# Output projection of two transformer layers as three products of split operands, in two phases over eight banks

## The chip, the cores and the metric

The kernel runs on one core of a Trainium2 chip. The metric is the device time of one execution in microseconds; three runs of the kernel before gave 2158.05, 2159.62 and 2159.68, median 2159.62. The core has five engines that run side by side and wait for each other by semaphores: TensorE (PE) for matrix products and transposes, VectorE (DVE), ScalarE (ACT), GpSimd (POOL) and SyncE (SP), which here issues most of the DMAs. Matrix products write to eight PSUM banks of 128 x 512 float32.

## The reference

A first block (mixing, attention, mixture of experts) is followed by a layer norm and two layers of a second kind, 512 rows of width 1024. The change touches these two layers alone:

```python
def hybrid_layer_2(x, p_i, positions, w_in, ..., w_o, ln1_g, ln1_b, w_gu, w_down, w_pg, w_pp, ln2_g, ln2_b):
    h = x @ w_in                                  # then split, rotated
    oa = swa_sink_attention(qa, ka, va, sinks)    # 8 windowed heads of 64
    ob = dsa_sparse_attention(qb, kb, vb, qi, ki, wi, k_top)   # 8 heads over selected keys
    mix = jnp.concatenate([oa, ob], axis=-1) @ w_o
    x = layer_norm_2(DN_ALPHA * x + mix, ln1_g, ln1_b)
    g, u = jnp.split(x @ w_gu, 2, axis=-1)
    ffn = (jax.nn.silu(g) * u) @ w_down
    ple = (p_i @ w_pp) * jax.nn.sigmoid(x @ w_pg)
    return layer_norm_2(DN_ALPHA * x + ffn + ple, ln2_g, ln2_b)
```

All is float32. A product may be done in float32 directly, or by splitting both operands into a high part (float32r, a cast) and a low part (the rest, a subtraction) and adding high x high, high x low and low x high.

## The kernel before, in words

The rows are T = 4 tiles of 128, the width C8 = 8 chunks of 128. A loop over the two layers stands in each engine's program, in the order written there; each engine works through its own list in order. `plan_layer` gives every use of a PSUM bank a place in advance: `u2.begin` makes PE wait until the bank's previous use is freed, `u2.full` tells the reader, `u2.read` waits for that, `u2.free` and `u2.evacuated` are the way back. `Sig` is a counting semaphore with its uses per layer.

Attention runs over 64 units (kind, tile, head), in the order: windowed ("a") tiles 1, 2, 3; selected ("b") tiles 1, 2, 3, 0; windowed tile 0. Units 40 to 47 are kind b, tile 3, and have 512 keys; units 48 to 63 have 128. For each pair of units PE makes the scores (L2285, mask products L2292 or L2296). DVE takes each unit's row maximum (L1829) and after the second the negated pair (L1834 or L1837). ACT makes the exponential (L1263) once the pair's negation is there. PE transposes the probabilities three units later (L2304), ACT copies them (`take_pt`, L1252), and PE multiplies them by the values one unit after (L2315). In ACT's list, unit n is: `take_pt(n - 3)`, then the exponential of n. After a group of eight, DVE divides and evacuates the output (`take_o`, L1849 and L1851). DVE also picks the largest index scores in this loop (`pick`, L1807, L1808), up to unit 37.

Then PE transposes the heads' outputs (`oT`, 8 chunks, L2216), ACT copies them to `HT` (L1180), and once all are there PE makes the output projection `mix` in float32 (L2343): for each tile and half width 8 products of 128 x 128 by 128 x 512. For each tile DVE adds the residual (L1897), takes the statistics (L1694, L1696), POOL the reciprocal root (L974, L975), and DVE normalises (L1700, L1702). PE transposes the tile (`x1T`), ACT casts the high part (`split_x1`, L1193) and DVE subtracts the low part (L1873). `w_pg` is loaded by SP after `p` and `w_pp` (L860 to L862), once oT 0 is full; ACT casts its 8 chunks (L1281) after tile 0's split and DVE subtracts them (L1907) after tile 2's normalisation. PE ends the stage with two transposes of p (`plT`), 16 products of p with `w_pp` in 8 banks (`pp`, L2357), tile 3's transposes, and the gate product (`pg`), already done as three products by `split_product` (L244 to L246). After it comes the feed-forward part, also split.

Of the kernel before, what the change touches and what calls it, by code (L numbers as in the profile page):

```python
# [6 lines left out]
P = 128  # L7
F32, F32R, BF16, I32 = mybir.dt.float32, mybir.dt.float32r, mybir.dt.bfloat16, mybir.dt.int32
ALU = mybir.AluOpType
# [29 lines left out]
IN2 = 1704  # L39
# [30 lines left out]
HEAD_TAPS = 87  # L70
FILLERS = 2
PICKS_A, PICKS_B, PICKS_C = 18, 29, 29
PICK_AT = [3, *range(7, 34, 2), 34, 35, 36, 37]
# [104 lines left out]
def plan_layer(before):  # L178
# [36 lines left out]
    b.next = 0  # L215
    for j in range(C8):
        b.take(("oT", j))
    for t in range(T):
        for half in range(2):
            b.take(("mix", t, half))  # L220
        if t:
            for half in range(2):
                b.take(("x1T", t - 1, half))
    for c in range(2):
        b.take(("plT", c))
    for t in range(T):
        for half in range(2):
            b.take(("pp", t, half))
    for half in range(2):
        b.take(("x1T", T - 1, half))  # L230
    for t in range(T):
# [17 lines left out]
def build(nc, i, out, stop=None):  # L249
    ctx = ExitStack()  # L250
    with ctx:
# [248 lines left out]
        PT2 = at(o + 4 * S, 3, S)  # L500
        assert o + 7 * S <= offB + C8 * sum(b - a for a, b in IN_CUTS[1:4])

        pg_hi = part("w_pg_hi", offB, C8, D)
# [9 lines left out]
        o = offB + C8 * IN2  # L513
        w_o2 = at(o, C8, D)
        gu_hi = [part(f"gate_up_hi{n}", o + 4 * D + n * 2 * D, 2, C8, P) for n in range(2)]
# [184 lines left out]
        y_xhi = Sig("x1_high_parts", 2 * T)  # L700
        y_ghi = Sig("w_pg_high_parts", C8)
        y_glo = Sig("w_pg_low_parts", C8)
        y_dhi = Sig("down_high_parts", FC)
# [48 lines left out]
        def _(sp):  # L752
# [79 lines left out]
            with sp.Fori(0, LAYERS) as l:  # L832
# [24 lines left out]
                sp.dma_start(lnB, of("ln1_b_2").rearrange("a n -> (a n)").partition_broadcast(P)).then_inc(d_ln1, 16)  # L857
                u2.read(sp, ("oT", 0), l)
                apart(sp)
                sp.dma_start(p_in, of("p_2").rearrange("l b (t p) n -> (l b p) t n", p=P)).then_inc(d_pp, 16)  # L860
                sp.dma_start(w_pp, of("w_pp_2").rearrange("a (c p) n -> (a p) c n", p=P)).then_inc(d_pp, 16)
                sp.dma_start(w_pg, of("w_pg_2").rearrange("a (p c) n -> (a p) c n", c=C8)).then_inc(d_pg, 16)  # L862
                u2.read(sp, ("mix", T - 1, 1), l)
# [127 lines left out]
        def _(act):  # L991
# [179 lines left out]
            with act.Fori(0, LAYERS) as l:  # L1171
# [74 lines left out]
                def take_pt(n):  # L1246
# [5 lines left out]
                    u2.free(act.copy(PT2[:, n % 3, 0:w], ps[:, 0:w]), ("pT", kind, t, h))  # L1252

                for n, (kind, t, h) in enumerate(UNITS):
                    w = width(n)
                    kk = 0 if kind == "a" else 1
                    if n >= 3:
                        take_pt(n - 3)
                    y_neg.wait(act, l, n // 2 + 1)
                    if n >= 4:  # L1260
                        u2.evacuated(act, ("pT",) + UNITS[n - 4], l)
                    ps = u2.read(act, ("s", kind, t, h), l)
                    u2.free(act.activation(Pr2[:, n % 4, 0:w], ps[:, 0:w], ACT.Exp, bias=nmx2[:, kk, t, h:h + 1],  # L1263
                                           scale=HD ** -0.5, accum_out=ls2[:, kk, t, h:h + 1]), ("s", kind, t, h))
                    if n < T - 2:
                        take_in(n + 2, 4)
                    if n in TURN_AT:
                        key = TURNED[TURN_AT[n]]
                        take_turned(key, turned[key])
                    if kind == "a" and h == 7:  # L1270
                        y_sinkd.wait(act, l, WINDOWED.index(t) + 1)
                        y_sinke.inc(act.activation(es2[:, t], es2[:, t], ACT.Exp))
                for n in range(len(UNITS) - 3, len(UNITS)):
                    take_pt(n)
                for j in range(C8):
                    take_turned(("oT", j), HT[:, j])
                split_x1(0)
                act.wait_ge(d_pg, 16 * (l + 1))
                apart(act)
                for c in range(C8):  # L1280
                    y_ghi.inc(act.copy(pg_hi[:, c], w_pg[:, c]))  # L1281
                for t in range(1, T - 1):
                    split_x1(t)
                for c in range(2):
                    take_turned(("plT", c), pT[:, c])
                for t in range(T):
                    for half in range(2):
                        take_turned(("pp", t, half), PLB[:, t, 512 * half:512 * half + 512])
                split_x1(T - 1)
                gate_up_high(0, 0)  # L1290
# [25 lines left out]
        def _(dve):  # L1316
# [402 lines left out]
            with dve.Fori(0, LAYERS) as l:  # L1719
# [123 lines left out]
                def take_o(kind, t):  # L1843
                    kk = 0 if kind == "a" else 1
                    u2.evacuated(dve, ("s", kind, t, 7), l)
                    if kind == "a":
# [5 lines left out]
                                              rl2[:, kk, t].unsqueeze(2).broadcast_to([P, 8, HD]), ALU.mult), ("o", kind, t))  # L1852

                for n in range(len(UNITS) + 3):
                    if n < len(UNITS):
                        row_max(n)
                    if n == 4:
                        u2.all_evacuated(dve, [("in", t, 4) for t in range(T)], l)
                        y_rot.wait(dve, l, 5)
                        rotate(heads_of(KB, 1, HD), [KBD[:, :, n:n + 1] for n in range(2)], c32, s32, 1, 32, copies=2)  # L1860
                    if n in PICK_AT:
                        pick(PICKS_C + PICK_AT.index(n))
                    if n >= 4 and (n - 3) % 8 == 0:
                        take_o(*UNITS[n - 4][:2])
                take_o(*UNITS[-1][:2])

                def split_x1(t):
# [24 lines left out]
                for t in range(T):  # L1892
# [9 lines left out]
                    if t:  # L1902
                        split_x1(t - 1)
                    if t == T - 2:
                        for c in range(C8):
                            y_ghi.wait(dve, l, c + 1)
                            y_glo.inc(dve.tensor_tensor(pg_lo[:, c], w_pg[:, c], pg_hi[:, c].bitcast(F32), ALU.subtract))  # L1907
                split_x1(T - 1)
# [40 lines left out]
        def _(pe):  # L1949
# [262 lines left out]
            with pe.Fori(0, LAYERS) as l:  # L2212
# [108 lines left out]
                for n in range(len(UNITS) + 4):  # L2321
# [8 lines left out]
                    if n in TURN_AT:  # L2330
                        turn_heads([TURNED[TURN_AT[n]]])
                for j in range(C8):
                    if j % 4 == 0:
                        u2.all_evacuated(pe, [("o", "ab"[j // 4], t) for t in range(T)], l)
                    turn2(("oT", j), [O2[:, j // 4, t, (j % 4) * P:(j % 4 + 1) * P] for t in range(T)])
                for j in range(C8):
                    u2.evacuated(pe, ("oT", j), l)
                pe.wait_ge(d_o2, 16 * (l + 1))
                for t in range(T):
                    for half in range(2):  # L2340
                        ps = u2.begin(pe, ("mix", t, half), l)
                        for m in range(C8):
                            ins = pe.matmul(ps[:], HT[:, m, t * P:(t + 1) * P], w_o2[:, m, 512 * half:512 * half + 512], start=m == 0, stop=m == C8 - 1)  # L2343
                        u2.full(ins, ("mix", t, half))
                    if t:
                        y_x1.wait(pe, l, t)
                        tile("x1T", t - 1)

# [4 lines left out]
                for t in range(T):  # L2353
                    for half in range(2):
# [3 lines left out]
                        u2.full(ins, ("pp", t, half))  # L2358
                y_x1.wait(pe, l, T)
                tile("x1T", T - 1)  # L2360
                y_glo.wait(pe, l, C8)
                u2.all_evacuated(pe, [("x1T", t, half) for t in range(T) for half in range(2)], l)
# [60 lines left out]
```

## Time and profile before

| | us |
|---|---|
| median of three runs | 2159.62 |
| profiled execution | 2162.41 |
| its span | 2160.3 |
| PE busy | 1968.9 (91%) |
| DVE busy | 1124.6 (52%) |
| ACT busy | 725.5 (34%) |
| POOL busy | 149.1 (7%) |

Times of the trace count from the start of the span. A busy time is the union of the records of an engine; matmul records overlap, so the duration of one is longer than its step in a row of them. A float32 matmul is recorded as two instructions. An idle time in brackets stands before the instruction, with the line that released it. The clock in the table of stretches is the one granted to PE, as a share of 2.4 GHz.

### The profile page before, as it was taken

The page shows a single profiled execution, that of the slowest core. Times are in us where ns is not written, and L with a number is a line of the kernel's source. Part 1 is how long each engine was busy: PE and PEld are TensorE (multiplying, and loading weights), DVE is VectorE, ACT ScalarE, POOL GpSimd, SP SyncE. Part 2 cuts the span into 40 slices and gives each one's busy share as a digit, 9 for nine tenths or more (in the row PEclk, how much of TensorE's full clock was granted, in tenths as well). Part 3 has the DMA queues.
Part 4 walks back from the last instruction along what each step waited for, and adds up shares of the span by engine and source line. Part 5 has one row for each costly group of instructions (what it writes and reads, how often), then busy time and mean ns, then how long its engine had stood idle before and what let it go on. Part 6 is the DMA issues. An engine that isn't in the chain of part 4 may idle for free.

```text
span 2160.3 us, 25297 instructions
## 1 busy us (share of the span) xinstructions
PE 1968.9 (91%) x8610; PEld 1397.3 (65%) x8614; DVE 1124.6 (52%) x1828; ACT 725.5 (34%) x1222; POOL 149.1 (7%) x157
## 2 busy tenths in 40 slices
PE   4997994799998698999999999999889999999995
PEld 2445644666665455655788887865566478888784
DVE  2787625688886788635222222367872522222235
ACT  2034421455554234533233332213353313333221
POOL 1000001133332100000000000010000000000001
PEclk9999996899999799999999999999999999999998
DMA  9162104699995700022033342250002103334220
GB/s 378 55 230 81 68 10 147 220 366 357 353 358 187 297 3 1 21 108 59 20 97 97 97 136 86 94 178 9 1 21 108 39 20 98 97 97 155 68 88 39
DMA packets 148060, 267.17 MB, mean 124 GB/s; under 512 B 11456, under 2 KB 108736, under 8 KB 134784
## 3 DMA queue, kind: packets, MB, share of 16 engines
q1 hardware_dynamic: 141776, 256.29, 33.6%
q0 software_dynamic: 6192, 9.70, 1.4%
q8 instruction: 51, 0.84, 0.2%
q14 instruction: 41, 0.34, 0.1%
HBM read 257.57 MB, written 20.97 MB: 129 GB/s over the span
## 4 chain that ended last, share of the span: by engine, by line
PE 78%; DVE 13%; issue 3%; ACT 2%; DMA 2%; POOL 1%; SPq 0%; DVEq 0%; ACTq 0%; POOLq 0%
PE bank L244 15%; PE bank L245 15%; PE bank L246 15%; PE bank L2343 5%; PE bank L2184 5%; PE bank L2228 5%; PE bank L2000 3%; DVE arena L1808 3%; PE bank L2089 2%; DVE arena L1807 2%; PE bank L1976 1%; PE bank L2315 1%; PE bank L2357 1%; DVE arena L1829 1%; DMA arena<-w_ada 1%
## 5 line engine op out<-in xcount | busy, mean ns | idle before, releaser
L244 PE MATMUL bank<-ht_hi,gate_up_hi 128*128 128x512 f32 x704 | 274.1, 389 | 2.8 <-ACT arena L1297 2.8
L245 PE MATMUL bank<-ht_lo,gate_up_hi 128*128 128x512 f32 x704 | 273.9, 389 | 0.0
L246 PE MATMUL bank<-ht_hi,gate_up_lo 128*128 128x512 f32 x704 | 273.9, 389 | 0.0
L2228 PE MATMUL bank<-arena 128*128 128x512 f32 (+3 forms) x640 | 194.9, 464 | 11.5 <-ACT arena L1186 6.4
L1623 DVE TENSOR_TENSOR expert_gate_up_lo<-expert_gate_up,expert_gate_up_hi 128x2048 fp32r<-128x2048 f32 x64 | 146.6, 2292 | 57.8 <-ACT expert_gate_up_hi L1113 55.2
L1884 DVE TENSOR_TENSOR arena<-arena,bank 128x512 f32 (+1 forms) x44 | 30.2, 687 | 272.0 <-ACT arena L1205 272.0
L2228 PEld LDWEIGHTS bank<-arena 128*128 128x128 f32 x640 | 114.7, 196 | 85.9 <-issue 64.3
L244 PEld LDWEIGHTS bank<-ht_hi,gate_up_hi 128*128 128x128 f32 x704 | 132.2, 188 | 31.2 <-issue 3.7
L246 PEld LDWEIGHTS bank<-ht_hi,gate_up_lo 128*128 128x128 f32 x704 | 132.2, 188 | 27.5
L245 PEld LDWEIGHTS bank<-ht_lo,gate_up_hi 128*128 128x128 f32 x704 | 132.2, 188 | 27.1
L1113 ACT CAST expert_gate_up_hi<-expert_gate_up 128x2048 fp32r<-128x2048 f32 x64 | 121.6, 1902 | 71.7 <-PE bank L246 71.6
L244 PE MATMUL bank<-down_hi,product_hi 128*128 128x512 f32 x352 | 138.2, 393 | 3.5 <-DVE arena L1884 3.5
L246 PE MATMUL bank<-down_hi,product_lo 128*128 128x512 f32 x352 | 138.1, 392 | 0.0
L245 PE MATMUL bank<-down_lo,product_hi 128*128 128x512 f32 x352 | 138.0, 392 | 0.0
L1878 DVE TENSOR_TENSOR gate_up_lo<-gate_up_whole,gate_up_hi 128x2048 fp32r<-128x2048 f32 x44 | 100.9, 2292 | 67.4 <-ACT gate_up_hi L1199 66.8
L1888 DVE TENSOR_TENSOR down_lo<-down_whole,down_hi 128x1024 fp32r<-128x1024 f32 x44 | 53.9, 1224 | 157.7 <-ACT product_hi L1213 157.7
L974 POOL TENSOR_SCALAR arena<-arena 128x1 f32<-128x1 f32 x20 | 23.1, 1157 | 1388.7 <-DVE arena L1696 1388.7
L2184 PE MATMUL bank<-arena 128*128 128x512 f32 x256 | 115.1, 592 | 0.7 <-ACT arena L1135 0.7
L2343 PE MATMUL bank<-arena 128*128 128x512 f32 x256 | 111.1, 593 | 1.7 <-ACT arena L1180 1.7
L244 PE MATMUL bank<-expert_gate_up_hi,window_hi 128*128 128x512 f32 x256 | 103.8, 405 | 2.8 <-DVE window_lo L1646 2.8
L1211 ACT CAST down_hi<-down_whole 128x1024 fp32r<-128x1024 f32 x44 | 46.1, 1048 | 164.1 <-PE bank L246 164.1
L245 PE MATMUL bank<-expert_gate_up_lo,window_hi 128*128 128x512 f32 x256 | 101.1, 395 | 0.0
(334 smaller groups left out, 3383.6 us busy)
## 6 DMA issues: line engine op xcount, KB each, us to landing
gate_up_whole<-w_gu SPq DMA_DIRECT2D x88, 512.0 KB, 5.1
expert_gate_up<-w_gate_e SPq DMA_DIRECT2D x32, 1024.0 KB, 6.9
expert_gate_up<-w_up_e SPq DMA_DIRECT2D x32, 1024.0 KB, 9.5
arena<-w_down_e SPq DMA_DIRECT2D x32, 1024.0 KB
down_whole<-w_down SPq DMA_DIRECT2D x44, 512.0 KB, 3.5
arena<-w_ada SPq DMA_DIRECT2D x5, 4096.0 KB, 20.6
arena<-w_in SPq DMA_DIRECT2D x4, 2048.0 KB, 16.0
arena<-w_o SPq DMA_DIRECT2D x2, 4096.0 KB, 13.0
```

The lines of the kernel that those rows point to most:

```text
L244: pe.matmul(ps, xh, wh, start=start, stop=False)
L245: pe.matmul(ps, xh, wl, start=False, stop=False)
L246: return pe.matmul(ps, xl, wh, start=False, stop=stop)
L1113: act.copy(ring_hi[half], ring[s][:, :, 4 * half:4 * half + 4]).then_inc(m_whi, 1)
L1623: dve.tensor_tensor(ring_lo[s][:, :, c4], ring[s][:, :, c4], ring_hi[half].bitcast(F32), ALU.subtract).then_inc(m_wlo, 1)
L1808: own.link(dve.match_replace(sc, top8, sc, TAKEN))
L1878: dve.tensor_tensor(gu_lo[s], gu[s], gu_hi[s].bitcast(F32), ALU.subtract).then_inc(f_lo, 1)
L1888: dve.tensor_tensor(dn_lo[f % 2], w_dn[:, f % DN_SLOTS], dn_hi[f % 2].bitcast(F32), ALU.subtract)
L2000: ins = pe.matmul(ps[:], w_in[:, c, c0 + m * P:c0 + (m + 1) * P], HT[:, c], start=c == 0, stop=c == C8 - 1)
L2184: ins = pe.matmul(bank[4 + 2 * (s % 2) + half][:], AT[:, s % 2, c], ring_d[s % 2][:, c, 512 * half:512 * half + 512], start=c == 0, stop=c ...
L2228: ins = pe.matmul(ps[:, 0:b - a], HT[:, c, t * P:(t + 1) * P], w_in2[j][:, c], start=c == 0, stop=c == C8 - 1)
L2343: ins = pe.matmul(ps[:], HT[:, m, t * P:(t + 1) * P], w_o2[:, m, 512 * half:512 * half + 512], start=m == 0, stop=m == C8 - 1)
```

## The change

The output projection becomes three products of split operands, as the gate product is. `w_o` is loaded as before. Its chunks 4 to 7 (`OUT_FIRST`, the selected heads) are split inside attention: at units 41, 43, 45 and 47 ACT casts one (`out_high`, after that unit's exponential) and DVE subtracts (`out_low`, after that unit's row maximum). Chunks 0 to 3 (`OUT_LAST`) are split after the heads. The low part is written in place of the loaded weight; the high parts lie in room that is free by then. The heads are transposed in the order 4 to 7, 0 to 3; ACT casts each to `HT_hi`, DVE subtracts to `HT_lo`, from the same bank.

The projection runs in two phases: for all eight (tile, half) banks the chunks 4 to 7, then for all eight the chunks 0 to 3. The x1 transposes of tile t come after tile t + 2 of the second phase, for tiles 2 and 3 inside the small products of p. On SP, `w_pg` is issued right behind `p` once the first transposed head is full, and `w_pp` waits until the first tile of the projection is full. ACT's casts of `w_pg` come ahead of all x1 splits, and DVE's subtractions of it ahead of the first evacuation of the projection.

```diff
+OUT_FIRST, OUT_LAST = range(4, 8), range(4)
+OUT_SPLIT_AT = {41 + 2 * k: m for k, m in enumerate(OUT_FIRST)}
...
-    for j in range(C8):
+    for j in [*OUT_FIRST, *OUT_LAST]:
         b.take(("oT", j))
     for t in range(T):
         for half in range(2):
             b.take(("mix", t, half))
-        if t:
-            for half in range(2):
-                b.take(("x1T", t - 1, half))
+    for t in range(T - 2):
+        for half in range(2):
+            b.take(("x1T", t, half))
     for c in range(2):
         b.take(("plT", c))
     for t in range(T):
         for half in range(2):
             b.take(("pp", t, half))
-    for half in range(2):
-        b.take(("x1T", T - 1, half))
+        if t % 2:
+            for half in range(2):
+                b.take(("x1T", T - 2 + t // 2, half))
...
-                u2.read(sp, ("oT", 0), l)
+                u2.read(sp, ("oT", OUT_FIRST[0]), l)
                 apart(sp)
                 sp.dma_start(p_in, of("p_2").rearrange("l b (t p) n -> (l b p) t n", p=P)).then_inc(d_pp, 16)
+                sp.dma_start(w_pg, of("w_pg_2").rearrange("a (p c) n -> (a p) c n", c=C8)).then_inc(d_pg, 16)
+                u2.read(sp, ("mix", 0, 0), l)
+                apart(sp)
                 sp.dma_start(w_pp, of("w_pp_2").rearrange("a (c p) n -> (a p) c n", p=P)).then_inc(d_pp, 16)
-                sp.dma_start(w_pg, of("w_pg_2").rearrange("a (p c) n -> (a p) c n", c=C8)).then_inc(d_pg, 16)
...
+                def out_high(m):
+                    act.wait_ge(d_o2, 16 * (l + 1))
+                    y_ghi.inc(act.copy(w_o2_hi[m], w_o2[:, m]))
...
+                    if n in OUT_SPLIT_AT:
+                        out_high(OUT_SPLIT_AT[n])
...
-                for j in range(C8):
-                    take_turned(("oT", j), HT[:, j])
-                split_x1(0)
+                for j in [*OUT_FIRST, *OUT_LAST]:
+                    ps = u2.read(act, ("oT", j), l)
+                    y_ghi.inc(act.copy(HT_hi[:, j], ps[:]))
+                for m in OUT_LAST:
+                    out_high(m)
...
+                def out_low(m):
+                    y_ghi.wait(dve, l, (OUT_FIRST.index(m) if m in OUT_FIRST else OUT_LAST_HI + OUT_LAST.index(m)) + 1)
+                    y_glo.inc(dve.tensor_tensor(w_o2_lo[:, m], w_o2[:, m], w_o2_hi[m].bitcast(F32), ALU.subtract))
...
+                    if n in OUT_SPLIT_AT:
+                        out_low(OUT_SPLIT_AT[n])
...
+                for k, j in enumerate([*OUT_FIRST, *OUT_LAST]):
+                    ps = u2.read(dve, ("oT", j), l)
+                    y_ghi.wait(dve, l, HEADS_HI + k + 1)
+                    ins = dve.tensor_tensor(HT_lo[:, j], ps[:], HT_hi[:, j].bitcast(F32), ALU.subtract)
+                    u2.free(ins, ("oT", j))
+                for m in OUT_LAST:
+                    out_low(m)
+                for c in range(C8):
+                    y_ghi.wait(dve, l, PG_HI + c + 1)
+                    y_glo.inc(dve.tensor_tensor(pg_lo[:, c], w_pg[:, c], pg_hi[:, c].bitcast(F32), ALU.subtract))
...
+                def mix(t, half, ms):
+                    key = ("mix", t, half)
+                    ps = u2.begin(pe, key, l) if ms is OUT_FIRST else bank[b2.where[key][0]]
+                    ts, cs = slice(t * P, (t + 1) * P), slice(512 * half, 512 * half + 512)
+                    for m in ms:
+                        ins = split_product(pe, ps[:], (HT_hi[:, m, ts], HT_lo[:, m, ts]), (w_o2_hi[m][:, cs], w_o2_lo[:, m, cs]),
+                                            m == OUT_FIRST[0], m == OUT_LAST[-1])
+                    if ms is OUT_LAST:
+                        u2.full(ins, key)
+
+                for ms in (OUT_FIRST, OUT_LAST):
+                    y_glo.wait(pe, l, 4 if ms is OUT_FIRST else C8)
+                    for j in ms:
+                        u2.evacuated(pe, ("oT", j), l)
+                    for t in range(T):
+                        for half in range(2):
+                            mix(t, half, ms)
+                        if ms is OUT_LAST and t > 1:
+                            y_x1.wait(pe, l, t - 1)
+                            tile("x1T", t - 2)
```

## Rows read from the trace of the kernel before

**Rows 1.** The page's part 4: shares of the chain that ended last.
```profile
PE 78%; DVE 13%; issue 3%; ACT 2%; DMA 2%; POOL 1%; SPq 0%; DVEq 0%; ACTq 0%; POOLq 0%
```
**Rows 2.** Grouped by form, PE: line, shapes, count | busy us, mean ns | idle.
```profile
L2343 PE MATMUL bank<-arena 128*128 128x512 f32 x128 | 55.5, 593 | 0.8 <-ACT arena L1180 0.8
...
L244 PE MATMUL bank<-w_pg_hi,ht_hi 128*128 128x512 f32 x64 | 25.3, 395 | 2.0 <-DVE ht_lo L1873 2.0
```
**Rows 3.** Timeline of PE, heads' transposes to gate product: start us, us, what.
```profile
934.46 5.80 PE L2216 MATMUL bank<-arena 128*128 128x128 f32 x32 [0.79 <-DVE arena L1851]
941.10 27.73 PE L2343 MATMUL bank<-arena 128*128 128x512 f32 x64 [0.83 <-ACT arena L1180]
...
1000.73 14.00 PE L2357 MATMUL bank<-arena 128*128 128x512 f32 x32 [0.90 <-ACT arena L1180]
1014.56 1.04 PE L2216 MATMUL bank<-arena 128*128 128x128 f32 x8
1017.55 0.49 PE L244 MATMUL bank<-w_pg_hi,ht_hi 128*128 128x512 f32 x1 [1.95 <-DVE ht_lo L1873]
...
1651.15 27.73 PE L2343 MATMUL bank<-arena 128*128 128x512 f32 x64 [0.83 <-ACT arena L1180]
```
**Rows 4.** Timeline of DVE, same stretch: one tile's steps and the gate split.
```profile
968.87 0.69 DVE L1897 SCALAR_TENSOR_TENSOR arena<-arena,bank 128x512 f32<-128x512 f32 x1 [6.18 <-PE bank L2343]
...
974.56 1.28 DVE L1873 TENSOR_TENSOR ht_lo<-bank,ht_hi 128x512 fp32r<-128x512 f32 x2
...
990.38 9.16 DVE L1907 TENSOR_TENSOR w_pg_lo<-w_pg_whole,w_pg_hi 128x1024 fp32r<-128x1024 f32 x8
```
**Rows 5.** Timeline of ACT, same stretch: the casts of the gate weight.
```profile
970.27 7.67 ACT L1281 CAST w_pg_hi<-w_pg_whole 128x1024 fp32r<-128x1024 f32 x8
```
**Rows 6.** Timeline of PE at the 512-key units: two pairs' scores, unit 45's values.
```profile
906.59 1.13 PE L2285 MATMUL bank<-arena 64*128 64x512 f32 x4
...
910.75 1.13 PE L2285 MATMUL bank<-arena 64*128 64x512 f32 x4
...
917.18 1.00 PE L2315 MATMUL bank<-arena 128*128 128x64 f32 x8
```
**Rows 7.** Timeline of DVE there: negation, output group, next two row maxima, negation.
```profile
905.80 0.17 DVE L1837 TENSOR_SCALAR arena<-arena 128x2 f32<-128x2 f32 x1
905.88 0.20 DVE L1849 RECIPROCAL arena<-arena 128x8 f32<-128x8 f32 x1
906.70 0.69 DVE L1851 TENSOR_TENSOR arena<-bank,arena 128x512 f32<-128x512 f32 x1 [0.62 <-PE bank L2315]
908.08 1.29 DVE L1829 TENSOR_REDUCE arena<-bank 128x1 f32<-128x512 f32 x2 [0.69 <-PE bank L2292]
909.40 0.17 DVE L1837 TENSOR_SCALAR arena<-arena 128x2 f32<-128x2 f32 x1
```
**Rows 8.** Timeline of ACT there: copy, exponential, copy, exponential.
```profile
905.08 0.48 ACT L1252 COPY arena<-bank 128x384 f32<-128x384 f32 x1 [1.07 <-PE bank L2304]
906.08 0.69 ACT L1263 ACTIVATE arena<-bank,arena 128x512 f32<-128x512 f32 x1 [0.53 <-DVE arena L1837]
...
906.76 0.58 ACT L1252 COPY arena<-bank 128x512 f32<-128x512 f32 x1
907.23 0.70 ACT L1263 ACTIVATE arena<-bank,arena 128x512 f32<-128x512 f32 x1
```
**Rows 9.** Stretches: length, busy PE, PEld, DVE, ACT, POOL, granted clock, DMA share, GB/s.
```profile
902.00:920.00 18.00, 17.95 (x143) 14.57 (x144) 6.64 (x19) 11.89 (x32) 0.00 (x0) 1.00 0.01 2
...
932.00:940.00 8.00, 7.12 (x39) 6.75 (x38) 0.72 (x2) 3.65 (x9) 0.00 (x0) 0.58 0.27 96
...
1017.00:1063.00 46.00, 44.63 (x192) 35.97 (x192) 7.51 (x10) 7.18 (x10) 0.00 (x0) 1.00 0.08 23
```
**Rows 10.** SP's timeline, then DMA issues by line: KB each, us to landing.
```profile
937.24 0.42 SPq L862 DMA_DIRECT2D w_pg_whole<-w_pg  x1
...
w_pg_whole<-w_pg SPq DMA_DIRECT2D x1, 4096.0 KB, 15.2
```

More of the change, by code:

```diff
@@ L501, in build @@
         assert o + 7 * S <= offB + C8 * sum(b - a for a, b in IN_CUTS[1:4])
+        o_turned = o - offB
         pg_hi = part("w_pg_hi", offB, C8, D)
@@ L513, in build @@
         o = offB + C8 * IN2
-        w_o2 = at(o, C8, D)
+        w_o2 = part("w_o_whole", o, C8, D, dt=F32)
+        w_o2_lo = part("w_o_lo", o, C8, D)
+        w_o2_hi = {**{m: part(f"w_o_hi{m}", offB + 9 * D + (m - 4) * D, D) for m in OUT_FIRST},
+                   **{m: part(f"w_o_hi{m}", H0 + m * D, D) for m in OUT_LAST}}
+        assert 9 * D >= o_turned + 7 * S and 13 * D <= C8 * IN2
         gu_hi = [part(f"gate_up_hi{n}", o + 4 * D + n * 2 * D, 2, C8, P) for n in range(2)]
@@ L700, in build @@
         y_xhi = Sig("x1_high_parts", 2 * T)
-        y_ghi = Sig("w_pg_high_parts", C8)
-        y_glo = Sig("w_pg_low_parts", C8)
+        y_ghi = Sig("w_o_heads_w_pg_high_parts", 3 * C8)
+        y_glo = Sig("w_o_w_pg_low_parts", 2 * C8)
+        HEADS_HI, OUT_LAST_HI, PG_HI, PG_LO = 4, 4 + C8, 2 * C8, C8
         y_dhi = Sig("down_high_parts", FC)
@@ L1281, in _ @@
                     y_ghi.inc(act.copy(pg_hi[:, c], w_pg[:, c]))
-                for t in range(1, T - 1):
+                for t in range(T - 2):
                     split_x1(t)
@@ L1288, in _ @@
                         take_turned(("pp", t, half), PLB[:, t, 512 * half:512 * half + 512])
-                split_x1(T - 1)
+                    if t % 2:
+                        split_x1(T - 2 + t // 2)
                 gate_up_high(0, 0)
@@ L1903, in _ @@
                         split_x1(t - 1)
[L1904 to L1907, printed above, removed]
                 split_x1(T - 1)
@@ L2331, in _ @@
                         turn_heads([TURNED[TURN_AT[n]]])
-                for j in range(C8):
+                for j in [*OUT_FIRST, *OUT_LAST]:
                     if j % 4 == 0:
@@ L2335, in _ @@
                     turn2(("oT", j), [O2[:, j // 4, t, (j % 4) * P:(j % 4 + 1) * P] for t in range(T)])
[L2336 to L2347, printed above, removed]
+                def mix(t, half, ms):
[17 more added lines that the diff above has]
+                            tile("x1T", t - 2)
                 pe.wait_ge(d_pp, 32 * (l + 1))
@@ L2358, in _ @@
                         u2.full(ins, ("pp", t, half))
-                y_x1.wait(pe, l, T)
-                tile("x1T", T - 1)
-                y_glo.wait(pe, l, C8)
+                    if t % 2:
+                        y_x1.wait(pe, l, T - 1 + t // 2)
+                        tile("x1T", T - 2 + t // 2)
+                y_glo.wait(pe, l, PG_LO + C8)
                 u2.all_evacuated(pe, [("x1T", t, half) for t in range(T) for half in range(2)], l)
```

## The prediction

> **What bounds the kernel now.** I read the chain of work that ended last first: TensorE (PE) carries most of it [rows 1], so a cut in PE work can pay only where PE is the last to be ready, and added work on ScalarE (ACT) or VectorE (DVE) costs only where PE then waits. The grouped instructions of two stretches give the price of the two product forms [rows 2]. The timeline of PE from the end of attention to the gate product shows a nearly unbroken PE [rows 3]: transposes of the heads, the output projection (64 float32 products, each recorded as two instructions), the x1 transposes, the small projection of p, and the gate product. The timelines of DVE and ACT over the same time show what follows each tile [rows 4, 5]. Then I read the three engines where the change puts new work into attention, at the widest units [rows 6 to 8]: PE is busy 17.95 of 18.00 us there, ACT 11.89 and DVE 6.64 [rows 9]. The second layer repeats the first 710.05 us later [rows 3], so a layer's sum counts twice.
>
> **Price of the products.** Before: 55.5 us for the 128 recorded instructions, 0.867 us a float32 product [rows 2]. After: 64 x 3 = 192 products of the gate product's shape and type. That stage has 64 of each of the three kinds; a record lasts 395 ns with its overlap [rows 2], so I take the stretch: 192 of them in 44.63 us of PE [rows 9], thus 0.2325 us each and 44.6 us in all. PE work falls by 10.9 us a layer. The row is the same operation on the same shapes, so I give this term no more than 0.5 us either way.
>
> By the Trainium skill ("FP8 and Floating Point Precision", section "TensorE Precision Notes") true FP32 takes four passes through the array. Three passes in place of four would save 55.5 / 4 = 13.9 us; this case's ratio, 0.867 to 0.2325, is 3.73 passes, so the trace agrees only roughly. With the page's figure the final estimate would be 6.0 us lower, 2145.8.
>
> **From the heads' transposes to the gate product, layer 0.** The transposes start at 934.46, 0.79 after a wait for the last windowed output [rows 3]. The selected heads now go first and need none of it: start 933.7, the 32 transposes at their 5.80 us, end 939.5. Their high part on ACT takes the place of a copy of equal size; the low part on DVE is one 128x512 subtraction, 0.65 us as in the x1 split (1.28 us for two [rows 4]). DVE has the last head of the first four split about 1.5 us after its transposes, some 938.2, so the first phase starts at 939.5 rather than 941.10. It takes 96 x 0.2325 = 22.3 us: 961.8.
> In the shadow of this phase, ACT does the last two heads, 4 weight casts (7.67 us for 8, so 0.96 each [rows 5]) to about 944, DVE 4 weight subtractions (9.16 us for 8, 1.145 each [rows 4]) to about 946. w_pg was issued at 937.24 and landed 15.2 us later [rows 10]. Its issue moves about 1.5 us ahead, and w_pp (1 MB of the 5.5 MB in that burst) is no longer in front: 948 to 951. ACT's 8 casts end at 956 to 959, DVE's 8 subtractions about a microsecond later. The first tile of the second phase is full at 961.8 + 12 x 0.2325 = 964.6. So the gate split, which before stood 9.16 us in DVE between tiles [rows 4], costs nothing; if the load came more than 3 us late, DVE would evacuate late by the excess. SP now waits for that tile before it issues w_pp, which PE wants only at about 987; no transfer behind it comes late.
> Second phase: 5.58 us a tile. Tiles end at 967.4, 973.0, 978.5; the x1 transposes (1.04 us as recorded, with the overlap at their end [rows 3]; I take 0.9) end at 979.4; the last tile 985.0, x1 transposes 985.9, p's two transposes 986.8. DVE is now what is late: from the evacuation of a tile's second half to its normalised rows it takes 974.56 - 968.87 = 5.69 us, the first half adds 0.65, the x1 split 1.3 [rows 4]. That is 7.6 us a tile against 5.58 (6.5 with x1's transposes) on PE. Tile 0 done 973.1; tile 1 979.5; split to 980.8; tile 2 987.1; split to 988.4; first half of tile 3 evacuated 989.1; tile 3 done 994.7. The first small product needs that bank (the plan gives it bank 6): it starts at 989.1, a new wait of 2.3 us. Then 14.0 us of small products [rows 3], 0.9 for tile 2's transposes: tile 3's transposes start at 1004.0. In the trace they start at 1014.56 and the gate product 2.99 us later at 1017.55 [rows 3]; kept so, the gate product starts at 1007.0. **Gain: 10.5 us a layer**, with bounds 9 (the DVE chain 1.5 worse) and 12.5 (the 2.3 us wait absent).
>
> **What attention pays.** At units 41, 43, 45, 47 ACT gets a 1024-column cast (0.96 us pitch, about 1.05 until a waiter sees it) and DVE the subtraction of it (1.15). The trace of before has no such pair here. The lower bound is nothing, if both lie in idle time; this counts as a loss or zero, since nothing is removed from this stretch. The idle shares invite that reading. But both engines work in order: the subtraction stands before the next two row maxima, and waits for the cast, which stands behind the exponential of the pair before. That closes a loop: row maxima, negation, exponential, cast, subtraction, next row maxima. One turn from negation end to negation end, by the rows: 0.11 to the exponential (905.97 to 906.08), 0.68 to the copy (906.76), 0.47 to the second exponential (907.23), 0.68 for it, cast 1.05, hand-over 0.1, subtraction 1.15, two row maxima 1.32 (908.08 to 909.40), negation 0.17 [rows 7, 8]. Sum 5.73 us, against PE's pair of 4.16 (906.59 to 910.75 [rows 6]).
> Followed through: the first cast fits the idle 1.07 us ahead of 905.08 [rows 8], its subtraction ends at 906.2 instead of leaving DVE free from 904.5, so the negation at 905.80 ends 1.7 late. At unit 43 the evacuation of a finished output group (reciprocal and multiply, 0.20 and 0.69, with the link between them 0.9 [rows 7]) stands behind the second subtraction too. The negation of 44/45 ends at 907.7 + 5.7 + 0.9 = 914.3 (before 909.57), that of 46/47 at 920.1, with the last cast from 922.0 to 923.0. PE's values of unit 45, in the trace at 917.18 [rows 6], need a probability copy behind this cast: 923.65. PE has used up its lead and is **6.5 us late**; one more copy on ACT makes 6.9. From there the narrow units run at their old pace and give nothing back. I take 6.7, with 3 (half of the loop hidden by lead that I count too small) and 9 (the loop plus slower handovers) as bounds.
>
> **Sum.** -10.5 + 6.7 = -3.8 us a layer, -7.6 for two. The profiled execution took 2162.4 us (span 2160.3), 2.8 above the median of the runs, 2159.6; its own sum gives 2154.8, and the same difference on the median gives **2152.0 us**.
>
> **Rivals.** (1) *The casts and subtractions are covered.* If the order on ACT leaves PE fed, attention pays at most 3 us a layer and the kernel gains 15 to 21 us: 2138.5 to 2144.6. For it: the idle shares [rows 9] and the first cast's 1.07 us hole. Against: DVE's wait sits ahead of row maxima that PE and ACT need next. Chance 0.20.
> (2) *TensorE falls to half clock in attention: slower.* In 932 to 940 the granted clock is 0.58 on average, that is partly 1.2 GHz, after PE's work had thinned; before, with 17.95 of 18.00 us busy, it is 1.00 [rows 9]. The loop thins PE to 4.16 of 5.73 us. If the clock falls there, each microsecond of full-clock PE work that is on the path costs one more. The gain of 3.8 us a layer is gone after 3.8 us of such work. Most of the 21 us of PE work from 912 to 934 would cost 6 to 12 more a layer: 2164 to 2176. Against it: while the loop is last, slower PE work partly fits its waits, and once it is saturated the clock comes back, as at 940. Chance 0.10.
> The Trainium skill ("TensorE: Matmul & The Clock Gate", section "A second HAM failure mode: psum-queue depth-cycling") tells of a kernel whose short idles between groups of matmuls made the gate oscillate. Followed here it would be rival 2; the rows show one such fall at the end of attention and do not show it in the wide units.
> (3) *Both prices land at their bad ends* (gain 9, loss 8 to 9, or one short fall of the clock): within 0.2%, 2156 to 2163. Chance 0.14.
> That the change does not do what it says I count within these: the operand layouts are those of the gate product.
>
> **Chances.** The forecast, 2147 to 2156, has 0.56, nearly all of it faster by over 0.2% (below 2155.3); 0.04 of it lies within 0.2%, about what a measurement of this kernel can tell from no change. Faster 0.52 + 0.20 = 0.72; same 0.04 + 0.14 = 0.18; slower 0.10. The range leaves out the lower end of rival 1 and all of rival 2: 2140 to 2162.
>
> **What would show it.** Right: 192 output products at 0.2325; the gate split finished before the first evacuation; a 2 us wait of the first small product on DVE; the stretch from the heads' transposes to the gate product near 73 us (83.1 before); PE idle 1 to 2 us at several points between units 43 and 49, released by ACT's copies, and DVE row maxima 5.7 us apart by pair. Wrong: an attention stretch as long as before, row maxima 4.2 us apart (rival 1), or a granted clock near one half between units 41 and 63 (rival 2). A w_pg load that lands after 954, or a phase that waits for a bank, would make the first term wrong.

## The result, and the profile after

The changed kernel takes 2169.64 us (median of 6 runs, 2167.97 to 2175.43), the kernel before 2159.65 beside it: ratio 1.0047, 95% interval 1.0035 to 1.0060, slower by 10 us. Forecast were 2152.0, with 2140 to 2162 as the range. The profiled execution took 2169.38 us, its span is 2167.6, so 7.3 more than the span before, and its mean granted clock 0.949 (0.962 before).

The projection itself went as the sum said. Grouped by form, its products in layer 0 (the counterparts of [rows 2]):

```profile
L247 PE MATMUL bank<-w_o_hi,ht_hi 128*128 128x512 f32 x64 | 25.1, 392 | 0.0
L249 PE MATMUL bank<-w_o_hi,ht_lo 128*128 128x512 f32 x64 | 24.9, 390 | 0.0
L248 PE MATMUL bank<-w_o_lo,ht_hi 128*128 128x512 f32 x64 | 24.9, 389 | 0.0
```

PE's timeline, in parts, from the heads' transposes to the gate product (against [rows 3]):

```profile
946.34 5.75 PE L2248 MATMUL bank<-arena 128*128 128x128 f32 x32
951.85 0.47 PE L247 MATMUL bank<-w_o_hi,ht_hi 128*128 128x512 f32 x1
...
1000.74 8.83 PE L2398 MATMUL bank<-arena 128*128 128x512 f32 x16 [2.40 <-DVE arena L1933]
1009.41 1.05 PE L2248 MATMUL bank<-arena 128*128 128x128 f32 x8
1010.29 7.03 PE L2398 MATMUL bank<-arena 128*128 128x512 f32 x16
1017.16 1.04 PE L2248 MATMUL bank<-arena 128*128 128x128 f32 x8
1020.00 0.47 PE L247 MATMUL bank<-w_pg_hi,ht_hi 128*128 128x512 f32 x1 [1.79 <-DVE ht_lo L1909]
```

From transposes to gate product it is 1020.00 - 946.34 = 73.66 us, where 83.09 stood before. The new wait of p's first product for DVE's evacuation is there, 2.40 us.

The loss lies in front of it. The same timeline at the wide units and after them (against [rows 6]):

```profile
905.00 1.13 PE L2317 MATMUL bank<-arena 64*128 64x512 f32 x4
...
907.73 1.10 PE L2347 MATMUL bank<-arena 128*128 128x64 f32 x8 [0.63 <-ACT arena L1263]
...
910.79 1.13 PE L2317 MATMUL bank<-arena 64*128 64x512 f32 x4
...
914.23 1.10 PE L2347 MATMUL bank<-arena 128*128 128x64 f32 x8 [1.33 <-ACT arena L1263]
...
916.33 1.85 PE L2347 MATMUL bank<-arena 128*128 128x64 f32 x8 [0.55 <-ACT arena L1263]
918.11 0.80 PE L2317 MATMUL bank<-arena 64*128 64x128 f32 x4
```

A pair of wide units takes 910.79 - 905.00 = 5.79 us (4.16 before), with short waits for ACT's probability copies. Then, from about 917, each group of eight value products takes 1.85 us where it took 1.1. The clock says why. Busy times and granted clock by stretch, columns as in [rows 9]:

```profile
904.00:916.00 12.00, 9.34 (x63) 6.35 (x60) 5.78 (x11) 6.44 (x14) 0.00 (x0) 1.00 0.00 0
916.00:920.00 4.00, 3.67 (x19) 3.16 (x19) 2.41 (x4) 1.71 (x5) 0.00 (x0) 0.56 0.00 0
920.00:948.00 28.00, 28.00 (x139) 24.22 (x139) 9.19 (x33) 13.64 (x56) 0.00 (x0) 0.50 0.01 2
948.00:952.00 4.00, 4.00 (x27) 4.00 (x26) 3.26 (x5) 2.97 (x7) 0.00 (x0) 0.67 0.72 264
952.00:976.00 24.00, 24.00 (x107) 19.83 (x107) 15.71 (x16) 12.35 (x14) 0.00 (x0) 1.00 0.36 154
```

PE is busy 9.34 of 12.00 us, then falls to 1.2 GHz (0.50) and stays there for 28 us, up to and into the heads' transposes, although it shows no idle time in them. It rises during these transposes (0.67 on average in 948 to 952; the projection begins at 951.85) and is at 2.4 GHz in the projection. Layer 1 has the same fall, 0.50 from 1640 to 1664, again ended inside the transposes, which start at 1661.85. In the kernel before, the clock fell only at the end of this part of attention ([rows 9], 0.58 in 932 to 940).

The balance, in us; a layer's stretches are cut at PE's scores of units 42/43, at the heads' transposes and at the gate product:

| | before, layer 0 / 1 | after, layer 0 / 1 |
|---|---|---|
| scores 42/43 to transposes | 31.47 / 31.55 | 44.94 / 44.14 |
| transposes to gate product | 83.09 / 83.00 | 73.66 / 72.67 |
| both | 114.56 / 114.55 | 118.60 / 116.81 |

This is +4.0 and +2.3 us. The span's other 1.0 us is the balance of stretches that the change does not touch: 1.6 less ahead of unit 42 of layer 0, 2.2 more between the first gate product and layer 1's unit 42, 0.4 more at the end. The spread of the same kernel from run to run is larger than that (2157.10 to 2161.97 in six runs of the kernel before).

### The profile page after: what moved, and what is told of

Read it like the earlier page. It is cut to its first block, busy times and chain, and to the rows that moved or that the text cites. A ratio compares the mean times of both kernels' runs of the same rounds, so it can differ in the third digit from the quotient of the medians.

```text
span 2167.6 us, 25637 instructions
## 1 busy us (share of the span) xinstructions
PE 1974.7 (91%) x8742; PEld 1443.0 (67%) x8742; DVE 1153.9 (53%) x1860; ACT 740.1 (34%) x1238; POOL 149.2 (7%) x157
## 4 chain that ended last, share of the span: by engine, by line
PE 76%; DVE 13%; issue 3%; DMA 3%; ACT 2%; POOL 1%; SPq 0%; DVEq 0%; ACTq 0%; POOLq 0%
PE bank L247 16%; PE bank L248 16%; PE bank L249 16%; PE bank L2216 5%; PE bank L2260 4%; PE bank L2032 3%; DVE arena L1828 2%; PE bank L2121 2%; DVE arena L1827 2%; DMA arena<-w_in 2%; PE bank L2347 2%; DVE arena L1849 1%; PE bank L2398 1%; PE bank L2008 1%; PE bank L2317 1%
## 5 line engine op out<-in xcount | busy, mean ns | idle before, releaser
L2260 PEld LDWEIGHTS bank<-arena 128*128 128x128 f32 x640 | 115.4, 198 | 85.3 <-issue 62.9
L2216 PE MATMUL bank<-arena 128*128 128x512 f32 x256 | 115.1, 592 | 0.7 <-ACT arena L1146 0.7
L2347 PE MATMUL bank<-arena 128*128 128x64 f32 x544 | 97.6, 313 | 19.4 <-ACT arena L1263 19.3
L2347 PEld LDWEIGHTS bank<-arena 128*128 128x128 f32 x544 | 86.2, 227 | 31.4 <-ACT arena L1263 22.8
```

The source lines that it names most:

```text
L2216: ins = pe.matmul(bank[4 + 2 * (s % 2) + half][:], AT[:, s % 2, c], ring_d[s % 2][:, c, 512 * half:512 * half + 512], start=c == 0, stop=c ...
L2260: ins = pe.matmul(ps[:, 0:b - a], HT[:, c, t * P:(t + 1) * P], w_in2[j][:, c], start=c == 0, stop=c == C8 - 1)
L2347: ins = pe.matmul(ps[:, h * HD:(h + 1) * HD], PT2[:, n % 3, k * P:(k + 1) * P], v, start=k == 0, stop=k == nk - 1)
```

## Experiments

In what follows, "attention's stretch" runs from the scores of units 42/43 to the heads' transposes, and "the stage" from these transposes to the gate product; two numbers are layer 0 and layer 1. Every ratio is to the kernel before, measured beside the run.

Theory: all of the loss is in attention; half of it is the closed loop of waits (cast, subtraction, row maxima) and half the clock that falls after the loop has thinned PE's work. Rivals: the load of casts and subtractions costs in any order; the projection stage's new order costs; the clock fell for another reason.

**Splits taken out of attention (e1).** In both loops over the units the call is removed, and all eight chunks stand behind the heads:

```diff
-                    if n in OUT_SPLIT_AT:
-                        out_high(OUT_SPLIT_AT[n])
...
-                for m in OUT_LAST:
+                for m in [*OUT_FIRST, *OUT_LAST]:
                     out_high(m)
```

> The change, with the casts and subtractions of chunks 4 to 7 of w_o taken out of attention and put behind the heads' splits. Theory A (what made the change slower sits in attention alone: the closed loop of cast, subtraction and row maxima, and the half clock that follows it): the 512-key units return to 4.2 us a pair, the stretch from the scores of units 42/43 to the heads' transposes to 31.5 us (44.9 in the changed kernel), at full clock; the first phase starts about 5 us later after the transposes than in the changed kernel, since 4 casts and 4 subtractions stand in front of it. About 2149 to 2154, faster than before. Rival B (the projection stage's new order costs the time: gate split first, DVE late, new waits): the time stays near 2170 or rises by the 10 us that the later start costs.

Measured: 2156.09 us, ratio to the kernel before 0.9983 (0.9966 to 0.9999). Attention's stretch is 30.61 and 30.03 us, 0.9 and 1.5 less than in the kernel before. The stage is 82.0 and 81.4: the first phase waits for DVE.

```profile
941.84 0.77 PE L247 MATMUL bank<-w_o_hi,ht_hi 128*128 128x512 f32 x1 [6.75 <-DVE w_o_lo L1874]
...
943.25 0.63 PE L247 MATMUL bank<-w_o_hi,ht_hi 128*128 128x512 f32 x1
```

That is 8.3 and 8.8 us more than in the changed kernel, not 5, and the time is 2 us above the range expected: the wait is 6.75 us (7.51 in layer 1) and the first products behind it are at half clock (records of the first kind, every third product, stand 1.28 us apart, 0.68 once the clock is full). The loss is in attention; but moving the work behind it gives back most of what the projection gains.

**Subtraction one pair later (e2).** Casts stay at units 41, 43, 45, 47; DVE's subtractions go to 43, 45, 47, 49, one pair of units behind their casts:

```diff
+OUT_LOW_AT = {43 + 2 * k: m for k, m in enumerate(OUT_FIRST)}
...
-                    if n in OUT_SPLIT_AT:
-                        out_low(OUT_SPLIT_AT[n])
+                    if n in OUT_LOW_AT:
+                        out_low(OUT_LOW_AT[n])
```

> The change, with each subtraction in attention one pair of units later (43, 45, 47, 49) and the casts left at 41, 43, 45, 47: the same work, but DVE never waits for a cast. Theory A1 (the loop of waits, not the load, is what attention pays): row maxima 4.2 us apart, PE fed, clock full, stretch from scores 42/43 to the transposes 31.5 to 33 us, time 2136 to 2142. Rival A2 (the load on ACT and DVE delays PE in any order): the stretch stays above 38 us, time 2155 or more.

Measured: 2136.63 us, ratio 0.9891 (0.9854 to 0.9928). Same work, other order, 33 us less than the changed kernel. The timeline of DVE shows the first three subtractions right behind a negation, without a wait; the fourth waits 0.46 us for its cast. PE in the same 12 us is busy all the time and at full clock:

```profile
904.03 0.17 DVE L1858 TENSOR_SCALAR arena<-arena 128x2 f32<-128x2 f32 x1
904.11 1.22 DVE L1877 TENSOR_TENSOR w_o_lo<-w_o_whole,w_o_hi 128x1024 fp32r<-128x1024 f32 x1
905.25 0.20 DVE L1870 RECIPROCAL arena<-arena 128x8 f32<-128x8 f32 x1
905.57 0.69 DVE L1872 TENSOR_TENSOR arena<-bank,arena 128x512 f32<-128x512 f32 x1
906.31 1.29 DVE L1850 TENSOR_REDUCE arena<-bank 128x1 f32<-128x512 f32 x2
907.64 0.17 DVE L1858 TENSOR_SCALAR arena<-arena 128x2 f32<-128x2 f32 x1
907.71 1.22 DVE L1877 TENSOR_TENSOR w_o_lo<-w_o_whole,w_o_hi 128x1024 fp32r<-128x1024 f32 x1
910.47 1.29 DVE L1850 TENSOR_REDUCE arena<-bank 128x1 f32<-128x512 f32 x2 [1.54 <-PE bank L2325]
...
914.98 1.23 DVE L1877 TENSOR_TENSOR w_o_lo<-w_o_whole,w_o_hi 128x1024 fp32r<-128x1024 f32 x1 [0.46 <-ACT w_o_hi L1268]
```
```profile
904.00:916.00 12.00, 12.00 (x96) 9.62 (x94) 8.94 (x16) 10.75 (x24) 0.00 (x0) 1.00 0.01 1
916.00:932.00 16.00, 14.68 (x121) 11.70 (x121) 7.06 (x30) 10.49 (x49) 0.00 (x0) 1.00 0.01 2
```

The stretch to the transposes is 30.26 and 30.23 us. It is shorter than before, by 1.2 and 1.3, though work was added; the heads no longer wait for the last windowed output, and the clock is full up to the transposes in both layers. The stage takes 72.06 and 72.03. So the load itself costs nothing here that the trace shows; the order did.

**More PE work in the loop (e3).** The order of the changed kernel, with one more 512-column product in each of units 44 to 49, written over by the real one:

```diff
+EXTRA = {n: 1 for n in range(44, 50)}
...
+                        for _ in range(EXTRA.get(n, 0)):
+                            pe.matmul(ps[:], turned["q" + kind, h // 2][p0:p0 + HD, t * P:(t + 1) * P], keys[p0:p0 + HD, 0:512],
+                                      start=True, stop=True)
                         pe.matmul(ps[:, 0:w], turned["q" + kind, h // 2]...
```

> The change, with one more 512-column score product per unit at units 44 to 49 (overwritten by the real one): PE work is added, about 0.53 us a unit at full clock, 3.2 us a layer, most of it into time in which PE waits; the loop of waits stays. Theory C (half of attention's loss is the clock, which fell because PE's work thinned): the clock stays at or near full from unit 44 to 63 and the kernel gets faster by 10 to 14 us than the changed one, 2156 to 2160. Rival D (the clock fell for another reason, or the thinning that matters is elsewhere): the clock still falls and the time is that of the changed kernel or up to 6 us more, 2170 to 2176.

Measured: 2155.81 us, ratio 0.9989 (0.9968 to 1.0010): 14 us faster than the changed kernel by adding work. In the profiled execution the clock is full from the loop to the projection, in both layers. Below are two stretches of layer 0 and, from PE's timeline, the scores of units 42/43 and the values of unit 45:

```profile
904.00:916.00 12.00, 10.36 (x73) 7.29 (x71) 5.99 (x10) 6.50 (x15) 0.00 (x0) 1.00 0.01 1
916.00:936.00 20.00, 17.61 (x141) 14.16 (x142) 9.01 (x33) 13.92 (x58) 0.00 (x0) 1.00 0.00 2
```
```profile
897.90 1.13 PE L2321 MATMUL bank<-arena 64*128 64x512 f32 x4
...
918.40 1.10 PE L2351 MATMUL bank<-arena 128*128 128x64 f32 x8 [0.55 <-ACT arena L1264]
```

DVE's row maxima are still 5.6 to 6.6 us apart by pair (901.19, 907.76, 913.40, 919.04), so the loop is untouched. The stretch is 36.92 and 36.28 us: 5.5 and 4.7 over the kernel before, with the loop and no fall, and 8.0 and 7.9 under the changed kernel, with the same loop and the fall. Against e2, where the clock is full and there is no loop, it is 6.7 and 6.1 over.

This profile is of the fastest of ten executions: 2144.60 us at a mean granted clock of 0.966. The slowest took 2165.36 at 0.953, and those between have their clocks between. So "full clock" and the 8 us a layer are shown for that execution; the median gain is 14 us, where this one is 25 us under the changed kernel. Where the clock falls in the other executions no profile shows.

**Attention's part alone (e4).** The kernel before with the four casts and subtractions, results unused:

```diff
+                    if n in OUT_SPLIT_AT:
+                        m = OUT_SPLIT_AT[n]
+                        act.wait_ge(d_o2, 16 * (l + 1))
+                        y_ghi.inc(act.copy(w_o2_hi[m], w_o2[:, m]))
...
+                    if n in OUT_SPLIT_AT:
+                        m = OUT_SPLIT_AT[n]
+                        y_ghi.wait(dve, l, m - 3)
+                        y_glo.inc(dve.tensor_tensor(w_o2_hi[m], w_o2[:, m], w_o2_hi[m].bitcast(F32), ALU.subtract))
```

> The kernel before, with only the four casts and four subtractions in attention added, their results unused (the subtraction writes over the cast's result; the projection stays in float32). Theory A: it costs 11 to 13 us a layer, 2182 to 2186, with row maxima 5.7 us apart at the 512-key units and the half clock after them. Rival B (attention pays 6 to 7 a layer or less and the rest of the loss is in the projection stage): 2172 or less.

Measured: 2190.2 us, ratio 1.0145 (1.0109 to 1.0181), 30 us more. The stretch is 45.8 and 44.6 us, +14.3 and +13.1 over the kernel before, with the clock at 0.50 from 916 to 948. The part is reproduced without anything of the projection's change. The cost was put too low, at 22 to 26 us: the two stretches pay 27.4 us together, nearly all of the 27.9 between the profiled spans.

**Free banks for p's products (e5).** On top of the later subtraction:

```diff
     for c in range(2):
         b.take(("plT", c))
+    b.next = 0
     for t in range(T):
         for half in range(2):
             b.take(("pp", t, half))
```

> As e2_subtract_one_pair_later, and the banks of p's products dealt anew: after p's transposes the first two row tiles of p take banks 0 to 3, free since the splits of x1 tiles 0 and 1, and not 6 and 7, which DVE frees last. Theory (the 2.40 us wait of the first of p's products is for the bank alone, and the slow products behind it, 8.83 us for 16 against 7.03, are a fall of the clock that this wait brings): 2 to 4 us less a layer than e2, 2128 to 2133. Rival (the wait only moves to x1's last transposes or to the next bank): within 1 us a layer of e2, 2135 to 2139.

Measured: 2134.15 us, ratio 0.9883 (0.9862 to 0.9904), the lowest median of all. The wait for DVE is gone (one of 1.01 us for ACT is left) and the first sixteen records take 7.13 us:

```profile
981.16 7.13 PE L2400 MATMUL bank<-arena 128*128 128x512 f32 x16 [1.01 <-ACT arena L1193]
...
998.76 0.47 PE L249 MATMUL bank<-w_pg_hi,ht_hi 128*128 128x512 f32 x1 [1.84 <-DVE ht_lo L1911]
...
1001.60 0.63 PE L249 MATMUL bank<-w_pg_hi,ht_hi 128*128 128x512 f32 x1
```

The stage takes 68.98 and 69.01, 3.0 less a layer than in e2, which is within the 2 to 4 expected, and the profiled spans are 5.6 us apart. But the medians are only 2.5 apart, 1 us above the range expected; the two were measured at different times and their intervals overlap, so e5 is not shown to be faster than e2 as a whole. Only the fall in p's products is gone: in layer 0 the gate product behind has one in both runs, with products of 0.63 us (at 1001.60 here, from 1005.39 in e2). That the 2.40 us wait caused the fall behind it is not shown either: in layer 0 of the run with wide products (e7, below) that wait is there and p's products run at full clock.

**Gate split back behind tile 2 (e6).** On top of the later subtraction, DVE only:

```diff
-                for c in range(C8):
-                    y_ghi.wait(dve, l, PG_HI + c + 1)
-                    y_glo.inc(dve.tensor_tensor(pg_lo[:, c], w_pg[:, c], pg_hi[:, c].bitcast(F32), ALU.subtract))
...
                     if t:
                         split_x1(t - 1)
+                    if t == T - 2:
+                        for c in range(C8):
+                            y_ghi.wait(dve, l, PG_HI + c + 1)
+                            y_glo.inc(dve.tensor_tensor(pg_lo[:, c], w_pg[:, c], pg_hi[:, c].bitcast(F32), ALU.subtract))
```

> As e2_subtract_one_pair_later, with DVE's subtractions of the gate weight back behind tile 2's normalisation (the casts stay ahead). Theory (at three products the projection is short enough that DVE's chain is last, so this move is part of the gain): tile 3's evacuation comes 9.2 us later and p's first products wait for it; 14 to 18 us more than e2, 2150 to 2155. Rival (PE's small products cover it, the move was not needed): up to 4 us more than e2, 2137 to 2141.

Measured: 2159.8 us, ratio 1.0000 (0.9982 to 1.0017): all of e2's gain is gone.

```profile
993.56 9.20 PE L2400 MATMUL bank<-arena 128*128 128x512 f32 x16 [11.48 <-DVE arena L1931]
```

The wait for the bank is 11.48 us, 9.1 over the 2.40 without this edit, as priced. The stage takes 81.5 and 81.9 us, 9.5 and 9.9 more. That is 19 us; the medians are 23 apart, where 14 to 18 was expected, and the rest is not explained (the profiled spans are 20.2 apart). The faster products are worth little unless DVE's work goes out of their way too.

**Wide products after the fall (e7).** The changed kernel with `EXTRA = {n: 1 for n in range(52, 56)}`.

> The change, with one more 512-column score product per unit at units 52 to 55, that is after the clock has fallen in the changed kernel (e3 put such products ahead of the fall). Theory (at half clock the narrow units keep it there although PE shows no idle time; it comes back with wide products, as it does at the projection): the granted clock is back at 1.00 within some 5 us of them, and the layer gains 2 to 5 us net of their cost, 2160 to 2166. Rival (the clock does not come back before the projection): 3 to 4 us of added half-clock work a layer, 2175 to 2178.

Measured: 2164.64 us, ratio 1.0015 (1.0002 to 1.0027). The clock by stretch:

```profile
916.00:928.00 12.00, 12.00 (x61) 11.14 (x61) 3.43 (x11) 6.23 (x18) 0.00 (x0) 0.50 0.00 1
930.00:940.00 10.00, 9.57 (x75) 7.01 (x71) 4.02 (x18) 6.11 (x30) 0.00 (x0) 0.91 0.01 3
942.00:948.00 6.00, 5.87 (x27) 5.68 (x28) 2.99 (x6) 2.81 (x6) 0.00 (x0) 0.51 0.14 32
```

It came back with these products (between 928 and 932) and fell once more before the transposes. In layer 1 it came back too (0.92 in 1648 to 1652) and stayed at 1.00 up to the transposes. Attention's stretch is 44.06 and 43.51 us, 1.0 and 1.2 under the changed kernel measured beside it (e8, 45.05 and 44.68). The stage is shorter too, by 1.2 and 1.9; in layer 0 p's products show no fall here and one there. These four add up to 5.2 us; the medians are 4.9 apart, but the profiled spans only 2.4, so other stretches differ by as much as this gain. The mechanism shows in both layers; what it gains in attention is only about 1 us a layer.

**The change again (e8)**, beside the last three.

> The changed kernel itself, beside the others on one chip: 2168 to 2172, half clock from about unit 46 to the heads' transposes in both layers by every theory.

Measured: 2169.55 us, ratio 1.0048 (1.0034 to 1.0062), with the same half clock from 916 to 948.

## Why the prediction was wrong

*Price of the products*: right. The first products step by 0.227 to 0.232 us, against 0.2325 taken.

*Transposes to gate product*: right, mechanism and size. Forecast 73.3 us, measured 73.66 and 72.67. The first phase started with the end of the transposes; w_pg was there 13.6 us after its issue and its subtractions were done 4 us before the first evacuation; the small products waited 2.40 us for the bank (2.3 forecast). Inside the stretch two errors of size cancel: the products were some 1 us faster in all (192 times about 0.005), and the first sixteen records of p's products took 8.83 us where 7.03 is full clock. The gate split in its new place costs nothing, as the text had it; left in its old place it costs 9.5 and 9.9 us a layer (e6), which the text did not price.

*The loop in attention*: right as a mechanism, and near in size. In the changed trace the timeline of DVE gives

```profile
903.61 1.23 DVE L1876 TENSOR_TENSOR w_o_lo<-w_o_whole,w_o_hi 128x1024 fp32r<-128x1024 f32 x1 [2.91 <-ACT w_o_hi L1267]
904.75 1.28 DVE L1849 TENSOR_REDUCE arena<-bank 128x1 f32<-128x512 f32 x2
906.07 0.17 DVE L1857 TENSOR_SCALAR arena<-arena 128x2 f32<-128x2 f32 x1
909.25 1.23 DVE L1876 TENSOR_TENSOR w_o_lo<-w_o_whole,w_o_hi 128x1024 fp32r<-128x1024 f32 x1 [3.02 <-ACT w_o_hi L1267]
...
912.64 0.17 DVE L1857 TENSOR_SCALAR arena<-arena 128x2 f32<-128x2 f32 x1
...
918.28 0.17 DVE L1857 TENSOR_SCALAR arena<-arena 128x2 f32<-128x2 f32 x1
```

The run is 1.59 us ahead of the trace before at unit 42, so the forecast of 907.7, 914.3 and 920.1 for the ends of these negations reads 906.1, 912.7, 918.5; measured are 906.24, 912.81, 918.45. DVE waits about 3 us for each cast. Forecast for unit 45's values was 6.5 us late; in e3, with the clock held, they stand 918.40 - 897.90 = 20.50 us after the scores of units 42/43, where the trace before has 917.18 - 902.99 = 14.19: 6.3 late. Up to the transposes e3 is 5.5 and 4.7 us longer than the kernel before, 6.7 forecast. The kernel before has a fall of the clock ahead of its transposes that e3 has not, which may account for the difference; it is not shown.

*The step that failed* is the term of attention in the sum. It had the loop alone, 6.7 us with bounds 3 and 9, and put the half clock in attention at nothing; that stood aside as rival 2, "TensorE falls to half clock in attention", chance 0.10. Measured, attention pays 13.5 and 12.6 us a layer (44.94 and 44.14 against 31.47 and 31.55), and 8.0 and 7.9 of it is the clock (changed kernel less e3's profiled execution). The rival's own price was right: 6 to 12 us a layer, 2164 to 2176, and it is 2170.

What argued against it was wrong: "once it is saturated the clock comes back, as at 940". In the changed trace PE shows 28.00 of 28.00 us busy at 0.50. The rise before 940 in the trace before came during the heads' transposes, and so does the rise in the changed trace; I took it as the rule for any full engine. At the narrow units a PE without idle time stayed at half clock to the end of attention. So the fall could not be counted as a short one, of the kind that the trace before shows in 898 to 902 (granted clock 0.60), with twenty microseconds of narrow work behind it.

The passage of the Trainium skill that I cited beside that rival ("TensorE: Matmul & The Clock Gate", section "A second HAM failure mode: psum-queue depth-cycling") tells of short idles of PE that made the clock oscillate. The trace agrees in part: PE's waits were short, none over 1.33 us, but between unit 44 and the transposes the clock fell once in each layer and stayed down.

The Trainium skill's four passes for true FP32 ("FP8 and Floating Point Precision", section "TensorE Precision Notes") would have put the projection's gain 3 us a layer higher than 10.9; the measured stage is at the rows' figure. The estimate by the page was also added up wrong: 2152.0 less 6.0 is 2146.0, not 2145.8.

## What to carry to other kernels

Before putting work into the idle time of two engines, look for a loop: when B waits for A's new work, and A's next turn needs what stands behind B's, the period is the sum of all members, however idle each is. Let the consumer lag by one turn (here 33 us for a lag of one pair). And before adding waits ahead of a long stretch of small products, price that whole stretch at half clock; here 12 us of thinned matrix work (9.34 us busy) came before 28 us at half clock.

## What the runs showed of the hardware that was not expected

- PE stayed at 1.2 GHz for 28 us with a busy time of 28.00 us, mostly in units of 128- and 64-column products, and returned to 2.4 GHz inside the heads' transposes (0.67 on average in 948 to 952, 1.00 after). Four extra 512-column products brought it back for about 10 us in layer 0, and up to the transposes in layer 1.
- It fell after a stretch in which PE made only short waits, none longer than 1.33 us in 904 to 916.
- Adding some 3 us of products a layer (0.96 us for a pair of units in e3, three pairs) made the kernel 14 us faster (2155.81 against 2169.64).
- Falls also moved between runs of the same stretch (in layer 0, the first sixteen records of p's products took 7.13 us in e7 and 8.83 in e8, with the same wait of 2.40 us). What sets that is open.
